# The down weights of the experts loaded from the GpSimd's DMA queue instead of the SyncE's

## What is computed

```
logits = (h @ router_w) + router_b
top_v, top_i = lax.top_k(logits, 2)
gates = softmax(top_v)
for e in range(8):
    y += combine[..., e:e+1] * swiglu(h, w_gu[e], w_down[e])      # swiglu: (silu(h@g) * (h@u)) @ w_down
x = x + gt_f * rmsnorm(y, g_post_ffn)
```

## Time and profile before

| | us |
|---|---|
| median of 3 runs | 1466.25 |
| the profiled execution's own time | 1464.35 |
| its span in the trace | 1462.6 |
| TensorE matmul busy | 1267.1 (87%) |
| VectorE busy | 750.8 (51%) |
| ScalarE busy | 324.3 (22%) |
| GpSimd busy | 42.0 (3%) |
| bytes read from HBM | 456.66 MB |

### The profile page before, as it was taken

The page is one execution under the profiler, slowest core; times in us unless marked ns, Lnnn a source line. Parts: engine busy times, 40 slices in busy tenths (PEclk is TensorE's granted clock), DMA queues, the critical chain, the costliest instruction groups (busy, mean ns, idle before and its releaser), DMA issues.

```text
span 1462.6 us, 38889 instructions
## 1 busy us (share of the span) xinstructions
PE 1267.1 (87%) x15885; PEld 802.6 (55%) x15885; DVE 750.8 (51%) x1108; ACT 324.3 (22%) x706; POOL 42.0 (3%) x43
## 2 busy tenths in 40 slices
PE   3898998999987689979988997999899799889940
PEld 1458966888876655535544553555455355445520
DVE  0687736777754545534443543444455344435422
ACT  1105644333333311111111111111111111111110
POOL 1010000000010120000000000000000000000001
PEclk8899999999998699989999998999999899989975
DMA  9985021888898047999999999999999999999943
GB/s 339 392 329 194 2 87 32 287 291 297 298 387 327 1 165 268 393 394 375 395 393 395 395 393 394 396 394 393 395 395 393 394 379 395 393 395 395 393 160 108
DMA packets 199498, 460.71 MB, mean 315 GB/s; under 512 B 9584, under 2 KB 34848, under 8 KB 199328
## 3 DMA queue, kind: packets, MB, share of 16 engines
q1 hardware_dynamic: 185296, 403.79, 74.3%
q0 software_dynamic: 13984, 56.49, 10.4%
q10 hardware_dynamic: 192, 0.08, 0.0%
HBM read 456.66 MB, written 4.59 MB: 315 GB/s over the span
## 4 chain that ended last, share of the span: by engine, by line
issue 64%; PE 27%; DMA 4%; DVE 3%; ACT 1%; POOL 1%; POOLq 0%; SPq 0%; DVEq 0%; ACTq 0%
PE ps L801 4%; PE ps L629 3%; PE ps L757 3%; PE ps L758 3%; PE ps L759 3%; DMA ctx_tok<-in_ctx 2%; PE ps L747 2%; PE ps L689 2%; DMA ada<-in_ada_w 1%; PE ps L594 1%; PE ps L678 1%; PE ps L912 1%; PE ps L670 1%; PE ps L669 1%; PE ps L666 1%
## 5 line engine op out<-in xcount | busy, mean ns | idle before, releaser
L937 PE MATMUL ps<-w_gu,consts_sb 128*32 128x256 f32 x8960 | 539.6, 393 | 73.2 <-DMA w_gu<-in_moe_w_gu 71.4
L937 PEld LDWEIGHTS ps<-w_gu,consts_sb 128*32 128x32 f32 x8960 | 282.4, 112 | 278.0 <-DMA w_gu<-in_moe_w_gu 83.8
L1604 DVE COPY w_dn<-w_next 128x2048 f32<-128x2048 f32 x280 | 329.9, 1221 | 0.0
L949 PE MATMUL ps<-w_dn,consts_sb 128*32 128x256 f32 x4512 | 274.8, 384 | 1.6 <-DVE w_dn L1604 1.6
L949 PEld LDWEIGHTS ps<-w_dn,consts_sb 128*32 128x32 f32 x4512 | 149.6, 112 | 103.7 <-issue 10.6
L1596 DVE TENSOR_TENSOR consts_sb<-consts_sb,ps 128x128 f32<-128x128 f32 x140 | 40.4, 288 | 297.2 <-ACT consts_sb L1198 287.8
L1198 ACT ACTIVATE consts_sb<-ps 128x128 f32<-128x128 f32 x140 | 38.9, 278 | 567.9 <-PE ps L937 567.9
L1600 DVE TENSOR_TENSOR y_all<-y_all,ps 128x256 f32 x140 | 59.0, 421 | 177.8 <-PE ps L949 177.8
L1288 DVE SCALAR_TENSOR_TENSOR ada_acc<-ada,cols,ada_acc 128x512 f32<-128x512 f32 x140 | 105.0, 750 | 4.0
L1418 DVE TENSOR_TENSOR f_lo<-f_raw,f_hi 128x2048 fp32r<-128x2048 f32 x33 | 75.5, 2292 | 54.2 <-ACT f_hi L1085 52.7
L1085 ACT ACTIVATE f_hi<-f_raw 128x2048 fp32r<-128x2048 f32 x33 | 63.2, 1917 | 70.2 <-DMA f_raw<-in_ffn_w_gu 57.7
(11 more groups left out here) (218 smaller groups left out, 967.2 us busy)
## 6 DMA issues: line engine op xcount, KB each, us to landing
w_gu<-in_moe_w_gu SPq DMA_DIRECT2D x224, 1024.0 KB, 14.9
w_next<-in_moe_w_down SPq DMA_DIRECT2D x112, 1024.0 KB, 13.2
ada<-in_ada_w POOLq DMA_DIRECT2D x23, 2048.0 KB, 9.9
f_raw<-in_ffn_w_gu SPq DMA_DIRECT2D x44, 512.0 KB, 6.8
f_raw<-in_ffn_w_down SPq DMA_DIRECT2D x11, 1024.0 KB, 5.0
wqkv<-in_attn_w_qkv SPq DMA_DIRECT2D x3, 2048.0 KB, 19.4
wo_sb<-in_attn_w_o SPq DMA_DIRECT2D x1, 4096.0 KB, 23.8
y_rows<-y_all SPq DMA_DIRECT2D x80, 32.0 KB, 1.5
```

Of the source, the lines that this page charges most:

```text
L937: mm = pe.matmul(ps[UNIT * t:UNIT * t + UNIT, GU_BANK, 0:2 * W], x_cur[:, k, :], gate_up_columns(w_gu[x], half, kk, t), start=(k == 0), st ...
L949: mm = pe.matmul(ps[UNIT * t:UNIT * t + UNIT, Y_BANK, 0:OW], m_actT[:, q % QW, q // QW, :], w_dn[:, q, OW * t:OW * t + OW], start=(q == 0) ...
L1604: dve.tensor_copy(w_dn[:, 2 * half:2 * half + 2, :], w_next[:, y, 2 * half:2 * half + 2, :]).then_inc(s[f"d_copied{half}"], 1)
```

## The change

`load_down` is taken out of the SyncE's program, gets the issuing engine as an argument, and is called by GpSimd. GpSimd issues d(0) and d(1) behind its loads for the pooling mixer, and after clearing `w_dn` and `y_all` it runs a loop over 54 steps of its own, with its own counting registers: wait for `d_copied1`, issue d(s+2). SyncE's `after_step` only waits for `gated` and issues g(s+3); it runs 53 times. The bytes, the buffers, the semaphores and the other engines' programs are the same.

```
+    def load_down(eng, y, e, step):
+        for half in range(2):
+            src = mdn_v[bass.ds(e, 1), :, bass.ds(step * (MS // P) + 2 * half, 2), :]
+            eng.dma_start(w_next[:, y, 2 * half:2 * half + 2], src.rearrange("e p k n -> p (e k) n")
+                          ).then_inc(s[f"d_in{y}{half}"], 16)
...
     @block.sync
...
-        sp.wait_ge(s["acc_ready"], (EARLY + L1_LATE) * KC)
-        load_down(0, 0, 0)
-        sp.wait_ge(s["poolmix_ready"], TB)
-        load_down(1, 1, 0)
...
-        def after_step(x, y, gate_up=True):
+        def after_step(x):
             next_count(sp, left, n, digit)
             sp.reg_add(gone, gone, n)
             at = place(step)
-            sp.wait_ge(s["d_copied1"], gone)
-            load_down(y, *at)
-            sp.reg_add(step, step, GU_SLOTS - DN_SLOTS)
-            if gate_up:
-                at = place(step)
-                sp.wait_ge(s["gated"], gone)
-                load_gate_up(x, *at)
-            sp.reg_add(step, step, 1 - GU_SLOTS + DN_SLOTS)
+            sp.reg_add(step, step, 1)
+            sp.wait_ge(s["gated"], gone)
+            load_gate_up(x, *at)
...
     @block.gpsimd
...
+        pool.wait_ge(s["acc_ready"], (EARLY + L1_LATE) * KC)
+        load_down(pool, 0, 0, 0)
+        pool.wait_ge(s["poolmix_ready"], TB)
+        load_down(pool, 1, 1, 0)
         pool.wait_ge(s["sqrt_ready"], NORM_MOE_PRE + TB)
...
+        with pool.Fori(0, (STEPS - DN_SLOTS) // DN_SLOTS):
+            for y in range(DN_SLOTS):
+                next_count(pool, left, n, digit)
+                pool.reg_add(gone, gone, n)
+                pool.wait_ge(s["d_copied1"], gone)
...
+                load_down(pool, y, pool.snap(e, min_val=0, max_val=E - 1), pool.snap(round_, min_val=0, max_val=MSTEPS - 1))
+                pool.reg_add(step, step, 1)
         pool.wait_ge(s["y_landed"], 1)
```

More of the change, by code:

```diff
@@ L383, in load_gate_up @@
                 sp.dma_start(w_gu[x][:, part], src.rearrange("e p k n -> p (e k) n")).then_inc(s[f"w_{x}{half}"], 16)
[L385 to L390, removed]
         load_gate_up(0, 0, 0, range(3))
@@ L420, in place @@
             return sp.snap(e, min_val=0, max_val=E - 1), sp.snap(round_, min_val=0, max_val=MSTEPS - 1)
-        sp.reg_mov(step, DN_SLOTS)
-        def after_step(x, y, gate_up=True):
+        sp.reg_mov(step, GU_SLOTS)
+        def after_step(x):
             next_count(sp, left, n, digit)
@@ L428, in after_step @@
             at = place(step)
-            sp.wait_ge(s["d_copied1"], gone)
-            load_down(y, *at)
-            sp.reg_add(step, step, GU_SLOTS - DN_SLOTS)
-            if gate_up:
-                at = place(step)
-                sp.wait_ge(s["gated"], gone)
-                load_gate_up(x, *at)
-            sp.reg_add(step, step, 1 - GU_SLOTS + DN_SLOTS)
-        CYCLE = GU_SLOTS * DN_SLOTS if GU_SLOTS % DN_SLOTS else GU_SLOTS
-        REFILLS = STEPS - GU_SLOTS
[L440 to L444, removed]
+            sp.reg_add(step, step, 1)
+            sp.wait_ge(s["gated"], gone)
+            load_gate_up(x, *at)
+        REFILLS = STEPS - GU_SLOTS
+        with sp.Fori(0, REFILLS // GU_SLOTS):
+            for slot in range(GU_SLOTS):
+                after_step(slot)
+        for slot in range(REFILLS % GU_SLOTS):
+            after_step(slot)
         sp.wait_ge(s["y_defined"], 16 * len(range(TOP_K * T, SLOTS, T)))
@@ L507, in _ @@
         pool.memset(y_all[:], 0.0).then_inc(s["y_cleared"], 1)
+        left = unit_counts(pool)
+        n, digit, gone, step, e, round_ = (pool.alloc_register(name) for name in (
+            "pool_n", "pool_digit", "pool_gone", "pool_step", "pool_e", "pool_round"))
+        pool.reg_mov(gone, 1)
+        pool.reg_mov(step, DN_SLOTS)
+        with pool.Fori(0, (STEPS - DN_SLOTS) // DN_SLOTS):
[3 more added lines that the diff above has]
+                pool.wait_ge(s["d_copied1"], gone)
+                pool.reg_mod(e, step, E)
+                pool.reg_div(round_, step, E)
+                load_down(pool, y, pool.snap(e, min_val=0, max_val=E - 1), pool.snap(round_, min_val=0, max_val=MSTEPS - 1))
+                pool.reg_add(step, step, 1)
         pool.wait_ge(s["y_landed"], 1)
```

## The result

Over 20 runs of each kernel the median fell from 1467.72 to 1459.81 us, ratio 0.995 with an interval of 0.9939 to 0.996: some 7 us faster, where 8.2 were predicted. One of the 20 runs of before took 2163.63 us, as no other did, and without it the median would be the same within 0.05 us. A later comparison gave 0.9951 (0.9935 to 0.9968). Direction and size of the medians were right, but one term of the sum was far off, the profiles show a smaller gain than the medians, and so the agreement in size is in part luck.

A forecast was written before the change was run, and what follows sets the result against it. DMAs bound the steps; SyncE's refills and 80 `y_rows` issues set the end. Terms -4.7 - 4.5 + 0 + 1 + 0 + 0 + 0 = -8.2 us: profiled 1464.35 to 1456.15, median 1458.0, range 1452 to 1472.

The forecast's parts named there:

- S: Moment SyncE is free of refills, 1388.69 us before the change; whatever moves it was to move the time one to one.
- Behind the last gate/up load: After g(55)'s issue SyncE no longer waits for VectorE's copy and issues d(55) before `y_rows`: 4.7 us off.
- Earlier start: At the stream's start g(4) no longer waits for the copy and d(3), so the unbroken stream begins 4.5 us earlier.
- Gaps: DMAs running short at the five-unit expert's end: earlier g(s+3) fills them or meets full buffers; 0, bounds 3.5 either way.
- Rate: Down weights on the software queue q0 change the stream's rate: 1 us more, bounds 0 and 15.1 us more.
- rival C: The stream runs at the rate of 2 KB rows, costing 8 us: 1466; chance 0.09.
- GpSimd's issue: GpSimd's issues of down weights, 0.56 us per 1 MB, two behind each copy, are covered by the stream in flight: 0.
- Writes behind a full queue: The first `y_rows` writes stand behind g(55) and may be held: 0 more, bounds 0 and 8.7 us.
- d(0), d(1): The first two down loads land 50 us or more before use on either engine: 0.
- Rival A: PE's stalls merge into longer ones and the clock falls, costing 1.7 to 3.5 us a round: +2 to +13; chance 0.16.
- Rival B: GpSimd's descriptor writing and VectorE's copies exclude each other, costing 8 us, so no change: 1466; chance 0.06.
- Rival D: At the end the full queue holds the first writes by 8.7 us, so no change: 1466; chance 0.07.

The follow-up runs named there:

- before_few_writes: The kernel before with `y_rows` written in 20 DMAs of four units (128 KB) instead of 80 of one (32 KB): 1437.76 us, ratio 0.9799.
- after_copy_once: The changed kernel with 20 writes of 128 KB, VectorE copying down weights once per step, not per unit, and d(s+2) ordered after that copy: 1425.31 us, 0.9716.
- before_copy_once: The kernel before, all loads on SyncE, with 20 writes of 128 KB and down weights copied once per step, not per unit: 1423.20 us, 0.9701.

## Why the prediction was right, and where it wasn't

In the profiles the time fell by 4.2 us (1464.35 to 1460.18): S by 4.9, the writes took 1.0 more, the tail behind them 0.3 less. The medians fell by 7.9. The second profile of the kernel after (1464.26 us) is only 0.1 us under that of before, and its S only 1.3. Most of this spread is when the experts start: from the end of the first five-unit expert's gate_up to S it is 834.1 us before and 831.3 in both profiles after, so 2.8 us of S are gained in either, and some 2 of the time, as the writes took longer. The profiled run of before lies 3.4 below its median, and before_few_writes, with the same stream, was dry for 3.8 us longer than before's profile; so I take the profile of before as one with few gaps. That is argued: no trace of a median run of before was taken, and some 6 of the 7.9 us have no row to show them. That the forecast of 8.2 met the medians is luck to that extent.

1. *Behind the last gate/up load*, -4.7: the time from the end of g(55)'s issue to `y_rows` went from 4.70 to 0.45 us, so -4.25. Shown, bar the 0.45 of SyncE's own instructions.
2. *Earlier start*, -4.5: the first byte's order went from 559.43 to 552.80. Of these 6.6 us 2.1 are the time at which the experts started in that run (the five-unit copy of round 0 ends at 557.1, not 559.2); the rest is the 4.5. In the second profile that copy ends at 560.7, 1.5 later, and g(4) is issued at 556.42, 3.0 earlier: again 4.5. Shown.
3. *Gaps*, 0, bounds 3.5 to either side: measured +7.3 (10.4 for 3.1). This is the term that failed. I had argued that g(s+3), issued six microseconds earlier, fills the gap. I had not asked what is on order when the five-unit expert gets the last of its gate/up weights: with their own queue the down weights are through early, and 8.4 MB, 21 us, don't last for the 26.6 us until its slot is free. The sentence on DMAs that can "meet full buffers" named the mechanism, and its bound was less than half of what it cost.
4. *Rate*, +1: -1.3, the 821.5 us of before from d(3) on, less its gaps, against 820.2. Where both queues carry weights, as in 584.5 to 588.5 us, the rate is 400 GB/s, with this split (the 390 over the whole stream, for 393, is the gap):

```profile
q0 software_dynamic: 262, 1.05, 66.9%
q1 hardware_dynamic: 271, 0.55, 36.3%
```

   The nearer row was indeed the 412; the upper bound of 15 us and rival C are out.
5. *GpSimd's issue*: 0.71 us apiece, not 0.56, and covered: PE never waits for a down product's copy but for 1.6 us in one place, as it did before.
6. *Writes behind a full queue*, 0 with bound 8.7: +1.0; the first write held SyncE 2.58 us where it had been 1.57:

```profile
L443 SPq DMA_DIRECT2D y_rows<-y_all x80: 321/321/2579, 1383.8 to 1435.9; - x80
```

7. *d(0), d(1)*: nothing waits for them.

So -6.6 (2.1 of them the earlier start of that run) +7.3 -1.3 -4.25 = -4.9 for S. If the kernel before has in most runs the 6.9 us of gaps of before_few_writes and not the 3.1 of its profile, that would hide the miss in the medians; no run shows it.

Two smaller readings were off as well. By the prediction's own numbers the last sum had 1437.6 - 1405.4 = 32 us of slack, not 20; before_few_writes gained 28. And PE's stalls did not get fewer: 25 before and 25 after.

**Rival A** had its mechanism right, and it took part in the gap of round 1. The waits of the kernel after, from 560 to 1430 us:

```profile
PEld ps L945 <- DMA w_gu<-in_moe_w_gu: 98.3, 25, 10.7
```

and windows over the stall of round 2 and over the two last ones of round 1:

```profile
772.00:783.00 11.00, 5.43 (x58) 2.61 (x62) 0.29 (x1) 0.69 (x2) 0.00 (x0) 0.53 1.03 400
649.00:666.00 17.00, 8.16 (x76) 3.56 (x80) 0.91 (x2) 0.69 (x2) 1.42 (x2) 0.61 1.04 395
```

From round 2 on PE stalls once for 10.4 to 10.7 us, as priced (10.4), and the granted clock is 0.53, nearly all at 1.2 GHz. But this costs next to nothing there: the DMAs go on at 400 GB/s, and the rounds take 128.1 us, where those of before took 127.3 to 129.6. The rival's error was to charge slower matmuls in each round to a stream that waits for them only in one. Round 1 took 135.6 us, for 129.6 before, and there 2.4 of the 8.0 dry us are slow matmuls behind a stall, near the 1.7 to 3.5 that the rival had given. It asked for more than four such rounds; there was one. I had the sum of the stalls as "about the same"; it rose from 83.8 to 98.3.

**Rival B** did not come about. The copies, 280 of them, are as long as in the earlier trace rows:

```profile
L1612 DVE COPY w_dn<-w_next x280: 1218/1220/1227, 520.7 to 1405.9; 128x2048 f32<-128x2048 f32 x140
```

GpSimd's 112 issues took 698 to 752 ns each. But this is no test of the lock-out that the Trainium skill describes in "SBUF — State Buffer", section "SBUF: two separate sides". Each pair of issues waits for a copy, starts 0.9 us behind its end, and is over 1.4 us later, while the next copy starts 1.96 us or more behind the pair's start: in no profile here does one of GpSimd's issues of the down weights overlap a copy. What would happen if they met, no run here shows; the kernel's own order keeps them apart, so the rival's condition was never met. **Rival D** took 1.0 of its 8.7.

## What to carry to other kernels

Before moving a load to another queue, count the bytes that are on order when the longest piece of compute starts, and set them against its duration; a queue of its own for the small tensor drains that one first and leaves less on order. Look at what stands between the last compute and the end: here 80 small writes stood behind a last sum with some 30 us of slack, and writing in larger pieces was worth four times the change (28 us against 7). Where a slot is held by a copy repeated for every unit, copying once frees it early, and that closed the gaps whichever queue was used.

## What the runs showed of the hardware that I had not expected

- With both queues at work each gets about the same number of packets (262 and 271), so the one with 4 KB packets moved 1.05 MB while that with 2 KB moved 0.55. The earlier trace rows had shown this already; what I had not expected is its effect, that the down weights are through before they are needed and leave less to come.
- Where both kinds of row are under way the rate is a little higher, 400 GB/s, than that of q1 alone with 2 KB rows, 387. Over 819 us two queues make no difference: after_copy_once with two and before_copy_once with one both move 394.
- An issue of 1 MB on GpSimd takes 0.71 us for the down weights, and 0.56 for another tensor.
